# Third group's row maxima from rounded 64-row operands, in a fused decoder block on one core

## The reference, cut to what matters

```python
ATT_GROUPS = ((128, 1), (512, 4), (2048, 16))      # (window, dilation), 8 heads of 64 in each group

def dilated_window_attention(q, k, v, window, dilation):
    ...
    s = jnp.einsum('brhcqe,brhcke->brhcqk', qb, kb) * (E ** -0.5)
    ...
    s = jnp.where(valid, s, -jnp.inf)
    m = jnp.max(s, axis=-1)
    p = jnp.exp(s - m[..., None])
    l = jnp.sum(p, axis=-1)
    o = jnp.einsum('brhcqk,brhcke->brhcqe', p, vb)
...
    ms = jnp.stack(maxes)
    wts = jnp.exp(ms - jnp.max(ms, axis=0))
    den = jnp.sum(wts * jnp.stack(dens), axis=0)
    num = jnp.sum(wts[..., None] * jnp.stack(outs), axis=0)
    o_b = (num / den[..., None]).reshape(B, S, ATT_DIM) * jax.nn.silu(ag.astype(jnp.float32))
```

## Time and profile before

| | us |
|---|---|
| median of 3 runs | 1509.67 (1508.07 to 1510.61) |
| the profiled execution | 1508.62 |
| its span (first to last instruction) | 1506.45 |
| TensorE busy | 1488.2 |
| VectorE busy | 854.9 |
| ScalarE busy | 705.1 |
| GpSimd busy | 33.3 |

### The profile page before, as it was taken

How to read it: one execution, slowest core, us unless ns; L and a number is a source line. 1 busy time by engine, 2 the same in 40 slices (tenths; PEclk the granted TensorE clock), 3 DMA queues, 4 the chain that set the end, 5 groups by cost and what they waited for, 6 DMA issues and landing times. The chain is left out here.

```text
span 1506.5 us, 21102 instructions
## 1 busy us (share of the span) xinstructions
PE 1488.2 (99%) x7927; PEld 1271.6 (84%) x7927; DVE 854.9 (57%) x1387; ACT 705.1 (47%) x877; POOL 33.3 (2%) x39
## 2 busy tenths in 40 slices
PE   7999999999999999999999999999999999999998
PEld 5888888888888888888888888888888888888987
DVE  6646555473646374667952586358635865644523
ACT  6646565665647474745522434344334435411212
POOL 1000000000000000001400000000000000000000
PEclk9999999999999999999999999999999999999999
DMA  5121111121111211122313212321232134332702
GB/s 217 43 70 57 53 46 69 56 70 56 53 58 56 70 45 66 56 70 71 89 53 87 68 36 79 86 70 33 81 85 70 31 105 135 118 119 100 263 29 84
DMA packets 35520, 116.84 MB, mean 78 GB/s; under 512 B 6200, under 2 KB 6520, under 8 KB 35448
## 3 DMA queue, kind: packets, MB, share of 16 engines
q1 hardware_dynamic: 35456, 115.94, 24.1%
HBM read 83.21 MB, written 20.02 MB: 69 GB/s over the span
## 5 line engine op out<-in xcount | busy, mean ns | idle before, releaser
L682 PE MATMUL z_ps<-h_hi,w_hi 128*128 128x512 f32 x1392 | 551.3, 396 | 0.6 <-ACT zz L1172 0.6
L684 PE MATMUL z_ps<-h_hi,w_lo 128*128 128x512 f32 x1392 | 542.8, 390 | 0.0
L683 PE MATMUL z_ps<-h_lo,w_hi 128*128 128x512 f32 x1392 | 542.2, 390 | 0.0
L684 PEld LDWEIGHTS z_ps<-h_hi,w_lo 128*128 128x128 f32 x1392 | 261.3, 188 | 55.6
L682 PEld LDWEIGHTS z_ps<-h_hi,w_hi 128*128 128x128 f32 x1392 | 261.7, 188 | 52.1 <-issue 1.6
L683 PEld LDWEIGHTS z_ps<-h_lo,w_hi 128*128 128x128 f32 x1392 | 261.8, 188 | 50.4
L1322 DVE TENSOR_TENSOR w_lo<-w_stage,w_hi 128x1024 fp32r<-128x1024 f32 x89 | 109.4, 1230 | 225.7 <-ACT w_hi L1012 225.2
L1020 ACT ACT_TABLE_LOAD x61 | 78.3, 1283 | 77.7 <-PE z_ps L684 77.0
L1120 ACT ACTIVATE pt<-pb 128x512 f32<-128x512 f32 (+1 forms) x80 | 43.4, 543 | 119.5 <-PE pb L828 119.2
L1012 ACT ACTIVATE w_hi<-w_stage 128x1024 fp32r<-128x1024 f32 x89 | 93.8, 1054 | 0.3
L845 PE MATMUL pc<-pt,vb 128*128 128x128 f32 x560 | 77.6, 279 | 1.2 <-ACT pt L1120 1.2
(11 more groups left out here) (257 smaller groups left out, 2202.6 us busy)
## 6 DMA issues: line engine op xcount, KB each, us to landing
w_stage<-w_in SPq DMA_DIRECT2D x88, 512.0 KB, 3.4
z_swap<-zz SPq DMA_DIRECT2D x96, 128.0 KB, 2.3
gate_d<-gate SPq DMA_DIRECT2D x16, 512.0 KB, 4.3
x_in<-x SPq DMA_DIRECT2D x8, 512.0 KB, 7.6
o_a_d<-o_a SPq DMA_DIRECT2D x8, 512.0 KB, 4.7
w_stage<-w_a SPq DMA_DIRECT2D x8, 512.0 KB, 3.8
cos_t<-gate_d SPq DMA_DIRECT2D x8, 512.0 KB, 4.6
sin_t<-gate_d SPq DMA_DIRECT2D x8, 512.0 KB, 3.6
```

Source lines behind the costliest of these rows:

```text
L682: nc.tensor.matmul(z_ps[hf][:], w_hi[s][:, k, :], h_hi[:, k, t], start=k == 0, stop=False)
L683: nc.tensor.matmul(z_ps[hf][:], w_hi[s][:, k, :], h_lo[:, k, t], start=False, stop=False)
L684: last = nc.tensor.matmul(z_ps[hf][:], w_lo[s][:, k, :], h_hi[:, k, t], start=False, stop=k == KT - 1)
```

## The change

The third group's maxima are computed from rounded operands with 64 rows, not from float32 operands padded to 128 rows.

- `q_sh[2]` is now of type f32r (its memory is read as float32 by the score products, as before). `k_hi2`, a new f32r tile in the memory of `zz[1]`, holds the rounded keys of both heads.
- Queries: VectorE adds into `zz[0]` with one instruction of 128 rows (slot 12), and SyncE copies each head's 64 rows to `q_sh[2][h]` by two transfers (`q2_copied`), put behind the swap of chunk 4 and ahead of the load of chunk 8's weights. In slot 14 ScalarE rounds them into the other head's tile, on the same rows (`q2_rounded`), where zeros stood before. The keys' ones and zeros are as before, so those rows still drop out of the score products.
- Keys: in slot 14 VectorE writes `k_sh[2][h]` as before, then adds once more into `k_hi2`.
- Maxima: `maxima_of_both` does blocks of both heads in turn, 16 matmuls in a pair, each with 64 rows of operands, head 0 from partitions 0 to 63 and head 1 from 64 to 127.
- ScalarE's take of chunk 6 (value chunk of group 0, into the memory of `zz[0]`) waits for `q2_copied` instead of `rope_sum`. GpSimd's zeros in `q_sh[2]` and its clearing of the row after each pair are gone, with TensorE's waits for them.

```diff
@@ attention, on SyncE @@
+                        if c == 5:
+
+                            if first(i):
+                                sp.wait_ge(oa_stored, 16 * HEADS)
+                                for s in range(2):
+                                    sp.wait_ge(gate_stored[s], 16 * HEADS)
+                            summed, scored = value(sp, i * 6 + 5), value(sp, i * N_UNITS)
+                            sp.wait_ge(const_in, 32)
+                            sp.wait_ge(rope_sum, summed)
+                            if prev:
+                                sp.wait_ge(st_made, scored)
+                            for h in range(2):
+                                rows = slice(EDIM * h, EDIM * (h + 1))
+                                sp.dma_start(q_sh[2][h][rows, :].bitcast(f32), zz[0][rows, :]).then_inc(q2_copied, 16)
@@ on GpSimd @@
-            for i in range(1, PAIRS):
-                seen, cleared = value(pool, i * N_UNITS), value(pool, i * 2 - 1)
-                pool.wait_ge(const_in, 32)
-                pool.wait_ge(st_made, seen)
-                nc.gpsimd.memset(q_sh[2][0][EDIM:EDIM + 1, :], 0.0).then_inc(row_cleared, 1)
-                pool.wait_ge(row_cleared, cleared)
-                nc.gpsimd.memset(q_sh[2][1][0:1, :], 0.0).then_inc(row_cleared, 1)
@@ on TensorE @@
+            def maxima_of_both(i, m):
+
+                pe.wait_ge(q2_rounded, i * 2 + 2)
+                pe.wait_ge(rope_sum, i * 6 + 6)
+                if max_bank(i, 2, m) is pc and not first(i):
+                    pe.wait_ge(ob_taken, i * N_SUMS)
+                else:
+                    pe.wait_ge(mx_taken, i * N_MAX + max_count(14 + 2 * m if first(i) else 16))
+                for blk, at, _ in max_queries(2, m):
+                    cols = slice(P * blk, P * blk + P)
+                    for h in range(2):
+                        rows = slice(EDIM * h, EDIM * (h + 1))
+                        last = nc.tensor.matmul(max_bank(i, 2, m)[:, h, at:at + P], q_sh[2][1 - h][rows, cols], k_hi2[rows, cols], start=True, stop=True)
+                        if blk == 4 * m + 3:
+                            last.then_inc(mx_made, 1)
@@ attention, on ScalarE @@
+                    if cur and slot == 14:
+
+                        act.wait_ge(q2_copied, i * 32 + 32)
+                        for h in range(2):
+                            rows = slice(EDIM * h, EDIM * (h + 1))
+                            nc.scalar.activation(q_sh[2][1 - h][rows, :], q_sh[2][h][rows, :].bitcast(f32), ACT.Copy).then_inc(q2_rounded, 1)
...
                             if g == 0 and hf == 0:
-                                act.wait_ge(rope_sum, i * 6 + 5)
+                                act.wait_ge(q2_copied, i * 32 + 32)
@@ attention, on VectorE @@
+                    if cur and slot == 12:
+
+                        dve.wait_ge(rope_a, i * 6 + 5)
+                        dve.wait_ge(rope_b, i * 6 + 5)
+                        nc.vector.tensor_tensor(zz[0][:], zz[0][:], z_swap[:], ALU.add).then_inc(rope_sum, 1)
+                    if cur and slot == 14:
+
+                        dve.wait_ge(rope_a, i * 6 + 6)
+                        dve.wait_ge(rope_b, i * 6 + 6)
                         if prev:
                             dve.wait_ge(st_made, i * N_UNITS)
                         for h in range(2):
                             rows = slice(EDIM * h, EDIM * (h + 1))
-                            dst = (q_sh, k_sh)[j % 2][2][h]
-                            last = nc.vector.tensor_tensor(dst[rows, :], zz[j % 2][rows, :], z_swap[rows, :], ALU.add)
-                        last.then_inc(rope_sum, 1)
+                            last = nc.vector.tensor_tensor(k_sh[2][h][rows, :], zz[1][rows, :], z_swap[rows, :], ALU.add)
+                        last.then_inc(k2_summed, 1)
+                        dve.wait_ge(k2_summed, i + 1)
+                        nc.vector.tensor_tensor(k_hi2[:], zz[1][:], z_swap[:], ALU.add).then_inc(rope_sum, 1)
```

## The result

The changed kernel is slower: 1521.16 us median (1520.25 to 1523.09) against 1509.76 for the kernel before, a ratio of 1.0079 (95% interval 1.0067 to 1.0091), some 11.4 us. The forecast of no change was wrong, and its range of 1503 to 1514 missed the time. Its profiled execution has a span of 1518.1 us (before: 1506.45).

What follows compares the result with a forecast made beforehand. TensorE, busy 1488.2 of 1506.5 us, was taken as the bound. Slot 16's gain of 8.6 us less 7.5 for the late rotation and 1.0 in pair 0 left 0.1 won: 1509.6 us, range 1503.0 to 1514.0.

Steps and rivals of the forecast that it cites:

- The forecast of no change: Whole kernel: 1509.6 us, its own range 1506.7 to 1512.7, given a chance of 0.50.
- The bound: Whole kernel: TensorE, busy 1488.2 of 1506.5 us, sets the time; other delays cost only what exceeds their slack.
- Gain in slot 16: Third group's maxima on TensorE: 2.15 us saved a pair (1.24 to 2.61), 8.6 us over four pairs (5.0 to 10.4).
- The spacing: Slot 16, between rounded 64-row matmuls: 0.07 us taken, between 0.06 and 0.112; 1.12 us a pair.
- the switch: Slot 16, going from 128 rows to 64 and back: 0.3 us a pair taken, from nothing to 0.54.
- How late the rotation comes: VectorE's keys' rotation, behind copies, chunk 8's weights and swap: 2.5 us late, at least 0.5, at most 2.9.
- That all of the delay becomes wait: Slot 14, pairs 1 to 3: no slack, so TensorE waits the full 2.5 us, 7.5 in all (1.5 to 8.7).
- Pair 0: Slot 16's first matmul waits for the low part of chunk 8's weights: 1.0 us lost once (0 to 1.4).
- The slack of 0.8 us: ScalarE's take of chunk 6's first half, before slot 14's matmuls: 0.8 us left after waiting for copies, less in pair 0.
- The sum: Whole kernel: 8.6 - 7.5 - 1.0 = 0.1 us won, giving 1509.6 us.
- The faster one: Copies at the weights' 369 GB/s, VectorE 1.5 us late: 4.1 us won, 1505.6 us; chance 0.32.
- The slower rivals: Slot 16: spacing stays 0.112 us and stream empties, 1513.2 us (0.14); or 64-row matmuls no faster than float32, 1518.2 us (0.04).

Runs made afterwards that it cites:

- e10: Changed kernel with the load of chunk 9's weights held back until the keys' half swap has landed: 1516.28 us.
- e2: Changed kernel with chunk 8's weights issued ahead of the wait for the query sum again, copies still before the swap: 1504.46 us.
- e9: Kernel before with only the load of chunk 8's weights made to wait for the query sum, right ahead of the swap: 1514.49 us.
- e7: Changed kernel with 14 extra unused matmuls in slot 14 of pairs 1 to 3, ahead of the maxima that wait: 1514.83 us.
- e12: Changed kernel with chunk 8's weights issued early and VectorE's row maxima of slot 13 put ahead of the keys' rotation: 1500.78 us.
- e4: Kernel before with only the query sum written to zz[0] and the two copies, ahead of chunk 8's weights and the swap: 1528.05 us.
- e3: Changed kernel with chunk 8's weights issued early and the two copies issued behind the keys' swap: 1516.38 us.
- e11: Changed kernel, transfers untouched, with VectorE's row maxima of slot 13 put ahead of the keys' rotation: 1510.18 us.
- e5b: Kernel before with the third group's maxima as float32 matmuls of 64 rows, written head by head: 1505.69 us, a single execution.

## Why the prediction was wrong, step by step

- **The bound.** Right. TensorE set the time, and each new wait showed in full.
- **Gain in slot 16.** Right mechanism, near size: 2.15 us a pair taken, 2.38 measured (9.4 in all, not 8.6). The spacing was 0.056 us a matmul (0.07 taken), the switch about 0.2 (0.3 taken). "TensorE: Matmul & The Clock Gate" (Part 3) in the Trainium skill has weight loads overlap where row groups differ, and the 0.112 us for two matmuls agrees. The Trainium skill's "TensorEngine Tiling (Array Packing)", Key Properties, has the engine drain at a change of mode: this trace shows a cost of 0.2 us, not the 0.54 that I had let the rule stand for.
- **How late the rotation comes: the step that failed.** 2.5 us, at most 2.9, against 4.1. What I left out is what is issued behind the swap: the load of chunk 9's weights, which in the longer queue cost 1.2 us in pair 1 and 0.7 to 1.2 over the four pairs (e10). I had read the queue only ahead of the swap. The terms I had, copies, weights and issue, are some 0.6 too small beside it: without that load the delay is 2.9 in pair 1 and 3.2 to 3.5 in the others (e10). Half of that is my working: data that end at 907.8 and the old tail of 0.6 (905.0 to 905.60) put the rotation at 908.4, 2.8 late, where I wrote 908.2 and 2.5.
- **That all of the delay becomes wait.** Right: delays of 1.1, 2.0 and 4.3 us (e2, e9, e7) lengthened slot 14 by 1.1 to 1.5, 1.8 to 2.0 and 4.0 to 4.5.
- **The clock.** Missing altogether: I priced a wait at its own length. The falls behind it cost 4.4 to 6.3 us (e7), as much as the mis-sized delay (3 x 1.6 = 4.8).
- **Pair 0.** 1.0 us taken, 2.7 measured: 0.93 in slot 13, where ScalarE's take waits for the copies, and 1.79 in slot 15 for the low weights, both named in the prediction and both sized too small. The slack of 0.8 us that I gave the take held in pairs 1 to 3 and not in pair 0.
- **The sum.** Forecast 0.1 won, the stage lost 10.8, a miss of 10.9: 4.8 for the delay, 4.4 for the clock, 1.7 for pair 0, less 0.8 of gain; 0.8 is rounding and small shifts.
- **The rivals.** The faster one rested on copies at 369 GB/s. The engines ran without a gap from 902.6 to 910.6 and moved 214, 320 and 238 GB/s in three stretches of it, 244 over the whole, 56% of the 435 GB/s of the Trainium skill's "DMA: Bandwidth & Descriptors", Where 436 GB/s comes from. The slower rivals looked for the loss in TensorE's slot 16; it was in the queue, and no rival went past 1518.2 us. The three stretches, windows of the kernel after:

```profile
902.60:905.90 3.30, 3.30 (x17) 2.71 (x16) 1.33 (x9) 0.00 (x0) 0.00 (x0) 1.00 0.94 214
906.00:907.50 1.50, 1.50 (x10) 1.26 (x9) 0.00 (x0) 1.09 (x2) 0.00 (x0) 1.00 0.96 320
907.50:910.60 3.10, 3.10 (x16) 2.52 (x15) 0.00 (x0) 1.49 (x2) 0.00 (x0) 1.00 1.02 238
```

## What to carry to other kernels

When a transfer is put into an in-order queue, list everything that now waits with it and everything issued right behind the transfer that is urgent: here a weight load that used to be issued 20 us ahead of the swap now waited for the query sum and then stood right ahead of the swap, and that cost more than the two copies themselves. Before pricing a wait, look for work that stands needlessly behind the late step on the waiting engine; moving four row maxima into VectorE's idle time was worth 3.7 us here (e2 to e12) and, with the load put back, turned a loss of 11 us into a gain of 8.5. And count a stall of TensorE at more than its length, since the clock may fall behind it.

## What the hardware showed that I had not expected

- The half clock does not follow the length of a wait alone. It came after waits of 3.2 to 3.7 us (all seven in the changed kernel, e4 and the first of e3), 2.4 to 2.9 (five of six in e3 and e10; one of 2.59 was without), and 1.73 twice in e11, while waits of 1.63 (changed kernel, pair 0), 1.36 (e11), 1.2 to 1.6 (e9) and 0.7 to 0.8 (e2) left it at 1.00. Each fall lasted 3.4 us, one 6.8; a fall of 3.4 us cost 1.6 to 1.9 us in e3.
- Matmuls on different halves of the rows overtake each other: in e5b a pc matmul starts at 924.11, before three pa matmuls that stand ahead of it in the program (924.22 and on).
- A load issued behind another transfer can slow it: 0.7 to 1.2 us in the changed kernel, nothing in e2, though in both a large part of it (0.47 to 0.53 and 0.28 to 0.40 of 0.52 MB) moved before the other had landed.
